# Streaming encoder layer on one core: choices 8 slots apart in groups 1 to 3, the sample's 12 apart, heads 16 apart, and turns of x placed between scores

## The reference

```python
h = rmsnorm(x, g_mix); proj = h @ w_in            # q,k,v,g (retention) and B,C,h (short conv)
x = x + concat([rms_scale(o) * silu(g), B * conv(C * h)]) @ w_out
# PEER, per token, on xn = rmsnorm(x, g_ffn):
q = (xn @ wq).reshape(T, 8, 2, 128)               # 8 heads, two half keys each
v1, i1 = top_k(q[:, :, 0] @ keys1, 16); v2, i2 = top_k(q[:, :, 1] @ keys2, 16)
top_s, sel = top_k(v1[..., :, None] + v2[..., None, :], 16)
eidx = (i1 * 128 + i2)[sel]; gate = softmax(top_s)
x = x + sum(gate * gelu(xn . u_tab[eidx]) * v_tab[eidx])
y = rmsnorm(x, g_final)
```

## Time and profile before

| | us |
|---|---|
| median of 3 runs | 3034.28 |
| the profiled execution, its own time | 3034.87 |
| its span, first to last instruction | 3033.1 |
| PE, VectorE (DVE), ScalarE (ACT), GpSimd (POOL) busy | 2306.7, 2072.1, 2026.1, 1245.7 |
| time in the chain that ended last: gathers into the ring | 36% |

### The profile page before, as it was taken

The page is one execution under the profiler, slowest core; times in us unless marked ns, Lnnn a source line. Parts: engine busy times, 40 slices in busy tenths (PEclk is TensorE's granted clock), DMA queues, the critical chain, the costliest instruction groups (busy, mean ns, idle before and its releaser), DMA issues.

```text
span 3033.1 us, 36677 instructions
## 1 busy us (share of the span) xinstructions
PE 2306.7 (76%) x12800; PEld 1885.1 (62%) x12800; DVE 2072.1 (68%) x5121; ACT 2026.1 (67%) x3690; POOL 1245.7 (41%) x1060
## 2 busy tenths in 40 slices
PE   9976887787768877876777777879777776666666
PEld 7765777665567766655566666665556555555555
DVE  2466887565688775666888744566588899954454
ACT  1277666667677666676677666667767777676666
POOL 0133433434433333444443344444434444555553
PEclk9987999898888899978887998899878886666666
DMA  7599999999999999999999999999999999999998
GB/s 300 187 417 401 411 411 411 417 420 412 420 419 409 409 420 419 419 403 420 420 417 408 393 418 419 419 419 404 411 420 419 419 413 414 414 418 411 421 420 338
DMA packets 180281, 1225.60 MB, mean 404 GB/s; under 512 B 20704, under 2 KB 21920, under 8 KB 40448
## 3 DMA queue, kind: packets, MB, share of 16 engines
q0 software_dynamic: 152064, 1107.36, 88.6%
q1 hardware_dynamic: 27744, 115.83, 9.6%
q10 hardware_dynamic: 288, 0.07, 0.0%
HBM read 1218.33 MB, written 4.86 MB: 403 GB/s over the span
## 4 chain that ended last, share of the span: by engine, by line
DMA 36%; DVE 23%; PE 22%; ACT 12%; issue 5%; POOL 1%; DVEq 0%; ACTq 0%; POOLq 0%
DMA ring<-in_uv,idx 36%; DVE ring L1495 11%; PE expert_sum L1146 9%; ACT ring L903 5%; PE mm L944 4%; PE x_ps L1006 2%; PE mm L1068 2%; PE mm L953 2%; ACT weights L899 2%; ACT L890 1%; DVE pairs_left L1342 1%; ACT dots L890 1%; PE expert_sum L944 1%; PE expert_sum L953 1%; DVE pairs_left L1430 1%
## 5 line engine op out<-in xcount | busy, mean ns | idle before, releaser
L682 POOL DMA_INDIRECT ring<-in_uv,idx x1056 | 1245.5, 1179 | 1765.2 <-PE expert_sum L1146 1549.8
L1146 PE MATMUL expert_sum<-ident_sb,ring 128*128 128x128 f32 x8448 | 1371.3, 318 | 579.7 <-ACT ring L903 576.5
L1495 DVE CUSTOM_DVE_ANT_0 ring<-ring,xn 128x1024 f32<-128x1024 f32 x1056 | 1286.2, 1223 | 730.4 <-DMA ring<-in_uv,idx 721.3
L1146 PEld LDWEIGHTS expert_sum<-ident_sb,ring 128*128 128x128 f32 x8448 | 1156.5, 165 | 836.5 <-ACT ring L903 761.5
L903 ACT ACTIVATE ring<-ring,weights 128x1024 f32<-128x1024 f32 x1056 | 1213.2, 1149 | 34.4
L890 ACT ACTIVATE dots<-dots 128x1 f32<-128x1 f32 x1056 | 211.5, 200 | 791.1 <-DVE dots L1495 784.7
L899 ACT ACTIVATE weights<-dots,gate 128x1 f32<-128x1 f32 x1056 | 311.1, 295 | 38.5 <-ACT dots L890 0.4
L944 PE MATMUL mm<-stream,xn_in 128*128 128x256 f32 (+1 forms) x912 | 259.6, 423 | 75.8 <-ACT qkvg L729 60.8
L1068 PE MATMUL mm<-turn,stream 128*128 128x256 f32 (+2 forms) x1024 | 279.1, 401 | 2.8 <-DVE xn_in L1185 2.8
L944 PEld LDWEIGHTS mm<-stream,xn_in 128*128 128x128 f32 (+1 forms) x912 | 168.4, 200 | 116.6 <-ACT qkvg L729 70.0
L1068 PEld LDWEIGHTS mm<-turn,stream 128*128 128x128 f32 x1024 | 190.7, 209 | 26.5 <-DVE xn_in L1185 3.1
(11 more groups left out here) (239 smaller groups left out, 1510.3 us busy)
## 6 DMA issues: line engine op xcount, KB each, us to landing
stream<-in_wq SPq DMA_DIRECT2D x36, 1024.0 KB
stream<-in_w_ret SPq DMA_DIRECT2D x26, 1024.0 KB
stream<-in_w_conv SPq DMA_DIRECT2D x24, 1024.0 KB
ring<-in_uv,idx POOLq DMA_INDIRECT x1056
ring<-in_w_ret SPq DMA_DIRECT2D x7, 1024.0 KB, 12.9
w_out_sb<-in_w_out SPq DMA_DIRECT2D x1, 4096.0 KB, 28.3
out_y<-xn SPq DMA_DIRECT2D x8, 512.0 KB, 14.6
x<-in_x SPq DMA_DIRECT2D x6, 512.0 KB, 10.1
```

The source lines that it names most:

```text
L682: pool.indirect_dma_start(ring[:, g % RING, :], None, uv, bass.IndirectOffsetOnAxis(ap=rows, axis=0)).then_inc(landed[g % RING], 16)
L1146: ins = pe.matmul(expert_sum[:, c * P:(c + 1) * P], ring[:, g % RING, D + c * P:D + (c + 1) * P], ident_sb[:, :], is_transpose=True, start ...
L1495: dve.tensor_tensor_reduce(u, u, xn[:, t % 3, :], 1.0, 0.0, ALU.mult, ALU.add, dots[:, g % RING:g % RING + 1]).then_inc(dotted, 1)
```

## The change

The passes of groups 1 to 3 start 16 slots apart for 15, and the second tile's keys and choices come 8 slots behind the first's for 7. The sample's choices are 12 apart for 7 (870 to 954 for 857 to 906 as starts). The turns of x move: in group 2 from 270, 274 to 270, 277; in group 3 from 526, 530, 534 to 526, 532, 536. The quads go from slot 936 to 996. Group 0 and the first turns stay.

```diff
-QUADS_AT = 7 * STEPS + 40
+QUADS_AT = 7 * STEPS + 100
...
-    return first_use_at(group_of(t)) - 10 + 4 * place(t)
+    j = group_of(t)
+    return first_use_at(j) + [(-10, -6), (-10, -6), (-10, -3), (-10, -4, 0)][j][place(t)]
...
-    PASSES += [(j, h, GROUPS[j], last_turn_at(j) + 5 + 15 * h, 2, 0) for h in range(PH)]
+    PASSES += [(j, h, GROUPS[j], last_turn_at(j) + 5 + 16 * h, 2, 0) for h in range(PH)]
...
-    return copy_at(n) + 1 + (3 if t == SAMPLE else 7 * PASSES[n][2].index(t))
+    return copy_at(n) + 1 + (3 if t == SAMPLE else (8 if PASSES[n][0] else 7) * PASSES[n][2].index(t))
...
-    return choose_at(PH - 1, t - 1) + 7 * (h + 1) if t == SAMPLE else scores_at(h, t) + 1
+    return choose_at(PH - 1, t - 1) + 12 * (h + 1) if t == SAMPLE else scores_at(h, t) + 1
```

## The result

The changed kernel takes 3052.89 us, median of 6 (3046.0 to 3055.34); the kernel before, in the same rounds, 3033.28. The ratio is 1.0061, 95% interval 1.0051 to 1.0070: 0.6% slower. A second series on another occasion gave 1.0049 (1.0035 to 1.0062). I had forecast 3030 with a range to 3039. The profiled execution has a span of 3053.5 us to the 3033.1 of before, with the same 36677 instructions and the same bytes.

A forecast was written before the change was run, and what follows sets the result against it. The DMA engines were taken to bound the kernel; 7.5 us gained less 2.7 lost left net 4.8, from 3034.9 to 3030.1, said as 3030. The range was 3021 to 3039, own range 3028.2 to 3036.

The forecast's parts named there:

- The bound: Whole run: DMA engines limit it, losing time only below 421 GB/s; touched windows lose 18.4 us together.
- Choices 8 apart: Choices of group 3 and the sample: parting Exp from a score copy gains 1.5 us, the sample's spacing 0.3.
- Exp ahead of the awaited copy: Three more Exps precede a projection copy PE awaits: 1.6 us lost in group 3, 0.4 each for two in group 2.
- all four waits of its sign: PE idle over 3 us before the projections of slots 284, 292, 316 and 572, after an Exp.
- The slower rival: Exp ahead of copies becomes the bound: three more cost stall 3.76 and slowed matmuls 1.47 us each; 3043 us, chance 0.12.
- The queues: SyncE's reordered loads in groups 2 and 3 keep enough lead, so none costs anything.
- Turns of x: Group 2: stalls at 271 and 276 go, gaining 1.7 us; group 3: 2.5 us gained, the keys' stall at 538 staying.
- the whole-gift rival: Stalls given back whole, group 3's turns giving 4.5 us; 10.7 us gained in all, 3024 us, chance 0.31.
- Slot 308: Group 2's projection: the wait stays but less work piles on it, gaining 1.5 of 2.1 us.
- Quads: Four ScalarE copies moved from slot 936 to 996: their 2.0 us loss moves, nothing saved.
- Last choices beside the convolution: Tile 3's last choices meet VectorE's convolution work from slot 352: 0.3 us lost, bounds 0 to 2.5.
- The Trainium skill's drain: ScalarE's table switches: the page's drain would add 2.4 us per Exp; the forecast held the trace has no such drain.

The follow-up runs named there:

- a1: Changed kernel with the prompt tiles' Exp one slot later, so ScalarE copies the scores of its slot first; ratio 1.0015 to the kernel before.
- c2: Changed kernel with the choices of tiles 2 to 7 one slot later and Exp kept in its slot; ratio 0.9998 to the kernel before.
- b6: Changed kernel with the second tile 7 slots behind the first again and tile 3's store ahead of the buffer's wait; ratio 1.0015 to the kernel before.
- c1: Changed kernel with choices, Exp and gates of tiles 2 to 7 one slot later; ratio 0.9989 to the kernel before.
- a2: Changed kernel with SyncE's store of tile 3's y at slot 519 for 520, ahead of the buffer's wait; ratio 1.0030 to the kernel before.
- d3: Kernel before with tile 3's store held until PE has done step 521; ratio 1.0011 to the kernel before.
- c3: Changed kernel with choices one slot later, Exp kept in its slot, tile 3's store ahead of the buffer's wait; ratio 0.9994 to the kernel before.
- d1: Kernel before with the choices of tiles 2 to 7, Exp and gates with them, one slot later; ratio 0.9991 to the kernel before.
- b3: Kernel before with only the sample's choices 12 apart and the quads at 996; ratio 0.9997 to the kernel before.
- e0: Changed kernel run again, unedited; ratio 1.0049 to the kernel before.
- d2: Kernel before with tile 3's store held until PE has done step 519; ratio 1.0000 to the kernel before.
- a6: Changed kernel with Exp one slot later, store ahead of the buffer's wait, norms of tiles 4 to 8 one slot earlier; ratio 0.9996 to the kernel before.

## Why the prediction was wrong, point by point

- **The bound** was right: the DMA engines, and a loss only where they run below 421 GB/s. The bytes and instructions stayed.
- **"Choices 8 apart" is the step that failed.** I priced a choice by VectorE's busy time (16.6 to 17.9 us for a pair's distance) and wrote that in group 3 the spacing "is to part Exp from a score copy: before, both are at the choice of the first tile + 6, after, Exp is one slot ahead of the copy", and took 1.5 us as a gain. The fact was right and its sign wrong; the wait of VectorE for that copy stood at nothing in my sum, without a reason. Within one slot ScalarE's list ran the copy first; parting them put 2.85 us of Exp before a copy that VectorE needs in the next slot. For this step I should have named what is queued behind the copy: the choice, and behind it the sweeps. Measured: 10 to 14 us when Exp goes back behind the copy (a1), 15 to 19 when VectorE gets a slot of slack (c2), for my 1.5 gained. In group 3, of which the sentence speaks, 2200 to 2760 us loses 10.6 us for 7.1 before, and 4.0 in c2.
- **"Exp ahead of the awaited copy"** named the right instruction and the right slots, and all four waits of its sign came, but it left out the other waiter. I priced the three new meetings at 2.4 us for PE's wait; c2 has PE's 3.74 us at slot 284 and the time of the kernel before. The 0.4 us each for group 2, where I took a stall to be cheap, was too low behind the stall at slot 277: the window 920 to 965 loses 7.4 us, and 8.7 in b6, where PE's wait is the long one. In the projection without choices beside it PE's wait does lose a little, 1.9 us at slot 564 before and 1.4 at slot 572 after (401 GB/s from 1760 to 1790), which is within what c1 and c2 differ by. The slower rival (0.12) had this same mechanism and was right in direction only.
- **"The queues"** failed too: I compared the leads of the weight loads and found them long enough, and did not ask what stands behind a load's *wait* in SyncE's order. The load of wq for the last head moved from 515 to 520, onto the store's slot. Measured 6 to 9 us with the other stalls about it (a2), 3.3 us for a stall of that size alone (d3).
- **Turns of x.** The stall before the keys at 271 went, as forecast, but in group 2 the norm at 267 now precedes the copy at 268, and the windows 880 to 965 lose 8.8 us, part of it at slot 284. In group 3 the keys of slot 538 wait 2.72 us, as forecast, and more was gained than my 2.5 us: slots 540 to 556 run at 421 GB/s. I had called a rise over 415 there a sign of being wrong, and it is: the whole-gift rival had this term right. The store's stall in front of it hid the gain. With the store out of the way slots 520 to 560 take 111.8 us in a2 and in c3 for 116.0 before; but the kernel before with the choices one slot later (d1) has 112.8 too.
- **Slot 308**: right there, 420 GB/s for 386. A smaller dip follows behind the Exp of slot 315, 408 GB/s from 1035 to 1070 (1.1 us lost, none before), so about 1 of the 2 us stays gained.
- **Quads**: in the changed kernel the 4.28 us cost 0.1 (the window 2885 to 2910 has 420 GB/s), where 2.0 were lost at slot 936. I said that they move; b3, whose total did not change, bears out only that it is too little to tell.
- **Last choices beside the convolution** were too cheap at 0.3 us: from 1150 to 1190 us (from slot 352 on) the changed kernel has 397 GB/s, 2.3 us lost (e0: 402, 1.8), where the kernel before has 419 from 1140 to 1180. That is near the upper bound of 2.5; how much of it is the Exps of slots 347 and 355 was not parted.
- **The Trainium skill's drain** (ScalarE: Activation LUTs, What ACT_TABLE_LOAD costs): the trace after disagrees as that of before did; from the start of the first load at 947.95 to the end of the second at 950.77 are 2.82 us. The change is a loss though a switch has no drain, and for another reason.
- **The range** ended at 3039. It was made of the prices of single stalls; it held nothing for stalls that meet.

## What to carry to other kernels

In an order written out by slots, a distance is also a phase: when a period is made to divide another (16 in 128, 8 in 16), a meeting can happen every time. For each moved piece ask what runs directly ahead of what it feeds, on that engine, and whether the consumer has a slot of slack; give a consumer on an engine that the ring waits for that slot before you spread its load. In a queue that runs ahead of its slots, look at the waits that a moved transfer brings, and what stands behind them. And price stalls by the pile: with seven buffers a lone wait of 4.8 us cost 3.3 (d3), one of 3.3 us nothing that could be told (c3), while five waits of VectorE within 110 us (850 to 960), 13.8 us together, and one of PE's of 3.74 went with 8.8 us lost.

## What was not expected of the hardware

Nothing of the hardware itself differed. A store of 512 KB took 7.8 us to land when issued 16 us behind a load of 1 MB (d2), and 8.4 when issued 8 us ahead of it (a6); issued 6.6 us behind it took 14.6 (before), 0.4 us behind it 15.8 (changed). PE's six matmuls after 3.74 us of idle time took 2.67 and 2.93 us for 1.46, as before, at the granted clock's lower level, 1.2 for 2.4 GHz, for all or most of them.
